# Two conditioning units of the prologue loaded into the weight ring, ahead of the tokens

## What is computed

```
c_act = silu(c)                                  # 1024
for l in range(2):
    mod = c_act @ ada_w[l] + ada_b[l]            # ada_w[l]: 1024 x 9216
    sh1, sc1, gt1, sh2, sc2, gt2, sh3, sc3, gt3 = split(mod, 9)
    h = rmsnorm(x, ffn1_norm[l]) * (1 + sc1) + sh1
    x = x + 0.5 * gt1 * swiglu(h, ffn1_w_in[l], ffn1_w_out[l])
    ...
```

## Time and profile before

| what | us |
|---|---|
| median of three runs | 2722.14 |
| the profiled execution | 2720.22 |
| its span | 2718.4 |
| PE busy | 2649.7 |
| DVE busy | 1865.9 |
| ACT busy | 1350.0 |
| first conditioning products on DVE | 10.48 |
| first feed-forward product on PE | 47.18 |

### The profile page before, as it was taken

The page is one execution under the profiler, slowest core; times in us unless marked ns, Lnnn a source line. Parts: engine busy times, 40 slices in busy tenths (PEclk is TensorE's granted clock), DMA queues, the critical chain, the costliest instruction groups (busy, mean ns, idle before and its releaser), DMA issues.

```text
span 2718.4 us, 52739 instructions
## 1 busy us (share of the span) xinstructions
PE 2649.7 (97%) x22179; PEld 2584.7 (95%) x22179; DVE 1865.9 (69%) x2544; ACT 1350.0 (50%) x1615; POOL 3.5 (0%) x7
## 2 busy tenths in 40 slices
PE   5899999999999999999999999999999999999998
PEld 5899889999998899999999989999999999999998
DVE  6888968878889556676555775565665655765654
ACT  3334654354456555564544636544555544655443
POOL 0000000000000000000000000000000000000000
PEclk8999999999999999999999999999999999999999
DMA  9897628978974355745455634355664456643552
GB/s 298 281 297 256 194 98 282 307 257 290 299 254 140 112 196 182 241 140 170 138 188 191 212 109 144 107 206 194 201 200 142 166 201 205 199 146 121 186 191 104
DMA packets 457930, 533.10 MB, mean 196 GB/s; under 512 B 9895, under 2 KB 434081, under 8 KB 457633
## 3 DMA queue, kind: packets, MB, share of 16 engines
q1 hardware_dynamic: 455920, 528.89, 59.2%
q10 hardware_dynamic: 1841, 1.88, 0.3%
HBM read 529.68 MB, written 2.63 MB: 196 GB/s over the span
## 4 chain that ended last, share of the span: by engine, by line
PE 87%; DVE 6%; DMA 3%; issue 2%; ACT 1%; SPq 0%; DVEq 0%; ACTq 0%
PE ps L2371 14%; PE ps L2189 13%; PE ps L2190 13%; PE ps L2191 13%; PE ps L2209 9%; PE ps L2880 6%; DMA work<-in_ada_w 3%; DVE work L1451 3%; PE ps L2672 2%; PE ps L2674 2%; PE ps L2673 2%; PE ps L2565 2%; PE ps L2410 2%; DVE wlo L1323 1%; PE ps L2850 1%
## 5 line engine op out<-in xcount | busy, mean ns | idle before, releaser
L1323 DVE TENSOR_TENSOR wlo<-raw,whi 128x2048 fp32r<-128x2048 f32 (+1 forms) x514 | 976.9, 1920 | 359.4 <-ACT whi L787 358.1
L787 ACT ACTIVATE whi<-raw 128x2048 fp32r<-128x2048 f32 (+1 forms) x514 | 827.9, 1616 | 426.5 <-PE ps L2191 143.4
L2189 PE MATMUL ps<-hhi,whi 128*128 128x256 f32 x1824 | 516.2, 283 | 2.7 <-issue 2.7
L2190 PE MATMUL ps<-hlo,whi 128*128 128x256 f32 x1824 | 505.9, 277 | 0.0
L2191 PE MATMUL ps<-hhi,wlo 128*128 128x256 f32 x1824 | 505.4, 277 | 0.0
L2189 PE MATMUL ps<-parts_f,whi 128*128 128x256 f32 x1344 | 372.0, 277 | 0.0
L2190 PE MATMUL ps<-parts_f,whi 128*128 128x256 f32 x1344 | 371.6, 277 | 0.0
L2191 PE MATMUL ps<-parts_f,wlo 128*128 128x256 f32 x1344 | 371.2, 276 | 0.0
L2371 PE MATMUL ps<-ghi,whi 128*128 128x256 f32 x1280 | 354.5, 277 | 7.5 <-DVE wlo L1323 7.5
L2189 PEld LDWEIGHTS ps<-hhi,whi 128*128 128x128 f32 x1824 | 344.1, 189 | 12.4 <-issue 12.1
L2371 PE MATMUL ps<-glo,whi 128*128 128x256 f32 x1280 | 354.2, 277 | 0.0
(11 more groups left out here) (304 smaller groups left out, 4537.6 us busy)
## 6 DMA issues: line engine op xcount, KB each, us to landing
raw<-in_ffn_w_in SPq DMA_DIRECT2D x88, 1024.0 KB, 10.4
raw<-in_ffn_w_gu SPq DMA_DIRECT2D x88, 1024.0 KB, 5.1
work<-in_ada_w SPq DMA_DIRECT2D x72, 1024.0 KB, 8.8
raw<-in_ffn_w_out SPq DMA_DIRECT2D x88, 512.0 KB, 6.3
raw<-in_ffn_w_down SPq DMA_DIRECT2D x88, 512.0 KB, 5.4
raw<-in_ca_w_kv SPq DMA_DIRECT2D x32, 1024.0 KB, 5.4
raw<-in_mix_w_in SPq DMA_DIRECT2D x24, 1024.0 KB, 5.4
raw<-in_da_w_in SPq DMA_DIRECT2D x24, 1024.0 KB, 5.8
```

Of the source, the lines that this page charges most:

```text
L787: f(whi[:, s, 0:size], raw[:, s, 0:size], ACT.Copy).then_inc(hi_done[s], 1)
L1323: tt(wlo[:, s, 0:size], raw[:, s, 0:size], whi[:, s, 0:size].bitcast(F32), ALU.subtract).then_inc(lo_done[s], 1)
L2189: mm(dst, wh, xh, start=first, stop=False)
L2190: mm(dst, wh, xl, start=False, stop=False)
```

## The change

Units 4 and 5 no longer use conditioning buffers 0 and 1. They are loaded into slots 0 and 2 of the weight ring, each with a semaphore of its own, right behind units 0 to 3 and without a wait; the tokens are issued after them. The loads of the first weight units into slots 0 and 2 now wait until DVE has summed units 4 and 5 (`ada_sum` at 48). The wait counts of the conditioning semaphores follow. From unit 6 on the loads and their waits are those of before.

```diff
--- before.py
+++ after.py
@@ -371,6 +371,7 @@
             "lower_done mix_f sgu_v sgu_s sgu_mm sgu_hi sgu_lo final_x final_mm final_c out_done").split()}
 
         ada_landed = [sem(f"ada_landed{i}") for i in range(ADA_BUFS)]
+        early_landed = [sem(f"unit_four_landed{i}") for i in range(2)]
 
         class Lane:
 
@@ -594,6 +595,18 @@
             return n
 
 
+        def raw_of(u):
+
+            if u in (4, 5):
+                return raw[:, 2 * (u - 4), :].rearrange("p (k m) -> p k m", k=KT)
+            return ada_raw[:, u % ADA_BUFS]
+
+        def landing(u):
+
+            if u in (4, 5):
+                return early_landed[u - 4], 16
+            return ada_landed[u % ADA_BUFS], 16 * (u // ADA_BUFS + (u < 4 or u % ADA_BUFS > 1))
+
         def summed(u):
 
             return 8 * u
@@ -676,6 +689,8 @@
                     s, use, src, size = plan.stream[sent[0]]
                     if use == 0 and s == 1:
                         sp.wait_ge(q["tok_turned"], 4)
+                    if use == 0 and s in (0, 2):
+                        sp.wait_ge(q["ada_sum"], summed(6))
                     if use == 0 and s == 3:
                         sp.wait_ge(q["line_out"], 16)
 
@@ -693,17 +708,17 @@
             def ada(u):
                 l, w = divmod(u, ADA_UNITS)
 
-                if u >= ADA_BUFS:
+                if u >= 6:
                     sp.wait_ge(q["ada_sum"], summed(2 * ((u - ADA_BUFS) // 2) + 2))
                 view = a["ada_w"][l].rearrange("(k p) m -> p k m", p=P)
-                load(ada_landed[u % ADA_BUFS], ada_raw[:, u % ADA_BUFS], view[:, :, 256 * w:256 * (w + 1)])
+                load(landing(u)[0], raw_of(u), view[:, :, 256 * w:256 * (w + 1)])
 
             for st in stages:
                 if st.kind == "prologue":
-                    for u in range(ADA_BUFS):
+                    for u in range(6):
                         ada(u)
                     load(q["token_in"], tok_x, a["x"].rearrange("o (t p) d -> p (o t) d", p=P))
-                    for u in range(4, 8):
+                    for u in range(6, 8):
                         ada(u)
                     stream(2)
                     for u in range(8, 10):
@@ -1436,14 +1451,14 @@
 
             def ada_pair(u, s=0):
                 for c in range(2):
-                    dve.wait_ge(ada_landed[(u + c) % ADA_BUFS], 16 * ((u + c) // ADA_BUFS + 1))
+                    dve.wait_ge(*landing(u + c))
 
                 if reduced[s]:
                     dve.wait_ge(q["ada_red"], reduced[s])
                 reduced[s] = u + 2
                 for k in range(KT):
                     for c in range(2):
-                        w, acc = ada_raw[:, (u + c) % ADA_BUFS, k, :], ada_acc[:, 2 * s + c, :]
+                        w, acc = raw_of(u + c)[:, k, :], ada_acc[:, 2 * s + c, :]
                         if k == 0:
                             m = ts(acc, w, silu_c[:, 0:1], None, ALU.mult)
                         else:
```

## The result

The changed kernel took 2726.63 us, the median of 17 runs (2723.95 to 2730.2), and the kernel before 2721.91 (2718.91 to 2723.73, 17 runs). The ratio is 1.002, with a 95% interval from 1.0014 to 1.0026: slower by 5.4 us, between 3.8 and 7.1. The two medians alone are 4.7 us apart. Forecast were 7.5 us and 2729.6.

The account below looks back on a forecast made before the run. PE's first feed-forward product, gated by prologue loads, bounds the start: 29.77 + 13.7 + 1.39 + 6.07 + 3.78 = 54.7 against 47.18, 7.5 us later. 2720.2 + 7.5 = 2727.7, on the median's level 2729.6; range 2724.0 to 2733.0.

Parts of the forecast that it names:

- Tokens: SP's load queue in the prologue: tokens, now the seventh megabyte, land at 29.8 us, where they landed at 19.63.
- the clean rate: Rival: queue runs at 350 GB/s, tokens land at 25.6, start 3.4 us later, 2725.5 us; chance 0.18, clean or nearly clean.
- Reading of the queue: DMA queue, 20 to 25 us: 294 GB/s against 350 afterwards, the difference put down to ACT's small loads.
- Units 4 and 5: SP's queue behind unit 3: both landed between 22.7 and 26.5; alone, their pair could start 3 to 7 us earlier.
- First gate: DVE's pair (4, 5) waits for PE's sum of pair (0, 1) behind the tokens' turns: starts at 35.0, idle 12 us.
- Second gate: DVE's `other_columns` waits for PE's late rows, ready 13.7 us after the tokens, at 43.5: another 2.4 us of waiting.
- The rest of the path: From late rows to PE's first product: `other_columns` 1.39 us, pair (6, 7) 6.07, then 3.78; start at 54.7.
- Weights: First weight unit issued at 41.1, ready at 48.2, wanted by DVE at 51.0: hidden, 2.8 us to spare.
- Clock: Rival at PE's first product unit: clock still up at 54.7, 2.2 us come back, 5.3 later, 2727.4 us; chance 0.08.
- Behind the start: Next steps of the first network: a circle of DVE, SP and conditioning load hands a late start on whole.
- Break-even: Tokens' landing at which the start equals the old one: 22.2 us, the start being the landing plus 24.9.
- The rival on the other side: SP's queue: tokens don't queue behind units 4 and 5, start 45.6, 1.5 us earlier, 2720.6 us; chance 0.03.

Follow-up runs that it names:

- e1: Changed kernel with the tokens issued fifth again, ahead of units 4 and 5, which stay in the ring; 2720.16 us, ratio 0.9998 to the kernel before.
- e2: Changed kernel with the tokens issued between unit 4 and unit 5; 2720.61 us, ratio 1.0 to the kernel before.
- e9: Changed kernel with ACT issuing its later 26 small loads only when the tokens have landed; 2728.36 us, one run.
- e4: Changed kernel with pair (4, 5) summing into an accumulator of its own, in space of silu_a; 2728.05 us, ratio 1.0031 to the kernel before.
- e10: The changed kernel once more, unchanged; 2726.7 us, ratio 1.0021 to the kernel before.
- e5: Changed kernel with PE's sums of pairs (0, 1) and (2, 3) ahead of the tokens' turns; 2726.82 us, ratio 1.0022 to the kernel before.
- e7: Changed kernel, PE order: sums of pairs (0, 1), (2, 3), tokens' turns, late rows, pair (4, 5), norm's sums, pair (6, 7); 2719.25 us, ratio 0.9995 to before.
- e8: Changed kernel with the late rows moved right behind the tokens' turns, ahead of PE's first pair sums; 2726.53 us, ratio 1.0017 to the kernel before.

## Why the prediction was right

The sign, the mechanism and the range (2724 to 2733) held. Step by step:

- *Tokens.* Predicted at 29.8, from the landing of the same megabyte; measured 29.34. The row was well chosen: the seventh megabyte lands between 29.34 and 29.87 in the kernel before, the changed one, e1 and e2. A landing at 25.6, the clean rate, did not come, and e9 shows what stood against it: with ACT's small loads out of the way the tokens land at 24.97. The Trainium skill's 358 GB/s (DMA: Bandwidth & Descriptors, Specifications) is met, 352 and 357 GB/s from 20 to 30 us in the changed kernel, and still the tokens come 3.8 us later than it gives, since the small loads and parts of units 6 and 7 were moved at that rate too.
- *Reading of the queue.* One step was wrong, without harm to the number. I put the 294 GB/s from 20 to 25 us down to ACT's small loads. The changed kernel moves 352 GB/s in that stretch with more of them in it (0.43 MB from 19 to 24 us, against 0.31). What was missing before was work in the queue: SP waited until 16.66 with unit 4, and e1, which issues it early, moves 4.60 MB from there to its unit 5's landing, where the kernel before moved 4.24. I also gave the whole delay to the small loads' share; their bytes are 1.7 us of it, and units 6 and 7 the larger part.
- *Units 4 and 5.* Predicted in between 22.7 and 26.5; e4 starts their pair at 25.88. The prediction gives no row for the upper bound.
- *First gate.* Pair (4, 5) predicted at 35.0 with 12 us of idle time; 34.70 and 11.56, released by PE (33.70 and 10.71 in e10). e4 and e5 open this gate and the pair starts at 25.88 and 26.42.
- *Second gate.* Copies of the late rows predicted at 43.5; 42.44. This is the term that was too large: I took 13.7 us from the tokens' landing to the end of the late rows, and it was 13.1 to their first copy. The norm's sums took 0.3 us less, and DVE begins before all eight turns are done. In e10, with PE's clock up earlier, it was 11.9, so the term itself scatters by more than I gave it.
- *The rest of the path.* 1.40, 6.07 and 3.78 us, as read. The start was predicted 7.5 us late and is 6.5: 0.4 from the tokens, 0.6 from the second gate. In e10 it is 5.2.
- *Weights.* Issue predicted at 41.1, ready at 48.2, with 2.8 us to spare; 40.88, 48.16 and 1.75. Hidden. With the tokens early it comes close: 0.3 us to spare in e1, 0.26 us of waiting in e2, whose starts (47.28 and 47.15) are within 0.1 us of that of before.
- *Clock.* The first product unit still began at the slow level (granted clock 0.51 from 53 to 58 us): its 48 records ran from 53.69 to about 61.4, 7.7 us against 8.09. Of the rival's 2.2 us 0.4 came. What the clock did change is what I hadn't priced, the sums ahead of the start, by 1.4 us between two executions.
- *Behind the start.* A late start is handed on whole: 6.5 and 5.2 us at the start, 5.4 (3.8 to 7.1) and 5.7 (3.3 to 8.2) at the end. The forecast of 7.5 lay above both, for the terms named. I had given 0.72 to a loss of over 5.4 us; the measured one lies just there, and its interval on both sides, so this is not decided.
- *Break-even.* Predicted at a landing of 22.2; e2 shows no loss at 23.57. From the tokens to the start I had 24.9 us; with PE's sums at their quick pace it is 23.1 (e10).

The rival on the other side (tokens not behind units 4 and 5, 1.5 us faster) had the right bound, the ninth megabyte at 35.8, and the wrong way to it. e7 reaches it with the tokens where the change put them.

## What to carry to other kernels

In a full queue, loading something earlier is a swap: name what lands later, and follow who waits for it on every engine, in order, before looking at what lands earlier. An engine with a fixed order turns one late input into a wait for work that doesn't need it; here two sums and the turns of the late rows stood behind the tokens for no reason of data. Where two gates stand one behind the other, opening either shows nothing, so open them together before calling one innocent.

## What I had not expected of the hardware

- The tokens' place in the queue cost 4.1 us for the first megabyte ahead (19.51 to 23.57) and 5.8 for the second (23.57 to 29.39), and without ACT's small loads about 5.3 for both (19.67 to 24.97). The small loads on ACT's queue, 0.5 to 128 KB each, cost the tokens 4.4 us, where their 0.61 MB are an estimated 1.7. Most of the rest is SP's own queue: about 1.06 MB of the two units issued behind the tokens was moved before the tokens' last bytes, and 0.25 MB without the small loads. A transfer's landing is that of its last part, and transfers issued behind it don't wait for that.
- PE's 16 records of the norm's sums took 6.30 us before, 6.03 and 5.41 in two executions of the changed kernel, 3.70 in e8, and 3.72 and 6.67 in two executions of the kernel of e7. The PEclk column reads 1.00 for 20 to 30 us in the earlier trace rows and for 20 to 42 in the stretches of the changed kernel above, where these sums took 6.03 us. Eight sums of a pair took 1.86 us in the kernel before at 36.08, under a column of 0.50, and 1.05 in the changed one at 42.71; the sixteen at 32.86 took 3.41, which is the slow level's pace, under a column of 1.00. As long as the column has not yet left 1.00 in a span it is no evidence of the fast level; durations are.
